# Last down matrices loaded and multiplied in three column parts, squares beside the copies, and the final norm's vector applied by feature

## The chip, the cores and the metric

The kernel runs on one core of one Trainium2 chip. The metric is the device time of one execution in microseconds (us), the median of several runs of the same program. Below, PE is TensorE, DVE is VectorE, ACT is ScalarE, POOL is GpSimd and SP is SyncE, which here only issues DMAs.

## The reference, cut to what matters

One step of a two-layer trunk over 256 prompt tokens and 8 sample tokens (264 columns in all, d = 1024). Each layer is a mixer (retention in layer 0, gated linear attention, GLA, in layer 1) and a mixture of 64 experts, eight of them for each token. The change sits at the end of both expert stages and in the norm after the second.

```python
def trunk(x, c, ...):
    for i in range(DEPTH):                       # DEPTH = 2
        sh1, sc1, g1, sh2, sc2, g2 = jnp.split(silu(c) @ ada_w[i] + ada_b[i], 6, axis=-1)
        h = modulate(x, norm_mix_g[i], sh1, sc1)          # rmsnorm(x, g) * (1 + scale) + shift
        m, S = mixer(h, ...)
        x = x + g1[:, None, :] * m
        h = modulate(x, norm_ffn_g[i], sh2, sc2)
        f = moe_ffn(h, ...)     # sum over 8 of 64 experts: w * (silu(h @ wg) * (h @ wu)) @ wd
        x = x + g2[:, None, :] * f
    return rmsnorm(x, final_norm_g), ...
def rmsnorm(x, g):
    return x * lax.rsqrt(jnp.mean(x * x, axis=-1) + EPS) * g
```

## The kernel before

**Layout.** The stream x lies feature by feature: eight chunks of 128 features (`k.x[:, c, :]`), each 264 columns, one for each token. Weights come from HBM through a ring of 12 slots of 1 MB. SP issues the loads in one fixed order, waiting for a slot to be free; `ring_full` and `ring_free` are its semaphores. All of them go through one hardware DMA queue.

**An expert stage.** Sixteen rounds of four experts. The last three rounds are light: each expert has at most 32 token slots, and the four of them stand side by side in one 128-row tile. In a light round PE computes gate (L2440), then spreads the round before back to the tokens, then up (L2440, L2557), turns the hidden tile (L2517), and multiplies by the four down matrices (L2450, weights 128x32, 512 columns at a time). ACT copies the rows out of PSUM.

**The last round** differs. Its down matrices come in two column halves (`rounds_sync`, L2350: four loads of 512 columns, then four more; `s_first_half` counts the first four). `pe_round` multiplies the first half into PSUM bank 6, ACT copies it (L3029), and `last_spread` (L2486) turns it into token columns, chunk by chunk: 128 features for each matmul, into two PSUM banks in turn, so that chunk c waits until DVE has added chunk c-2. The add is `add_last` on DVE, three instructions (L2859, L2861, L2864). After four chunks PE multiplies the second half into bank 7, ACT copies it, and the last four chunks follow.

**What follows each chunk.** PE puts `follow(c)` between the chunks. In layer 0 this is `nxt.sum` (L543), the sum of the squares for the next norm; ACT makes the squares (L526) after its second copy. In layer 1 it is `final_rows` (L1951): three transposes for each chunk (128, 128 and 8 tokens) put x by token into PSUM banks 2 to 7.

**The end of layer 0.** After the sums PE computes one block of conditioning vectors (L478), DVE and ACT finish the norm (L560, L532, L562, L569, L537), and the GLA projections (L1394) start on the first of twelve 1 MB loads of `gla_w_in`. SP has issued these behind the last down loads, two small loads (`gla_w_a`, L1335 and L1336) and four of `ada_w` (L303).

**The end of the program** (`final`). ACT squares the token rows out of PSUM with a running sum (L1959, four times 512 columns), and the samples by feature (L3433); PE sums the samples' squares (L1967). DVE puts the means together (L1999 to L2001), ACT takes the root (L1987), DVE the reciprocal (L2004). DVE then makes four blocks of 128x512 outputs, each the rows times their factor times the norm's vector (L2010); SP stores each (L2031). The samples go another way: ACT scales them (L1989), POOL multiplies by the vector (L2018), ACT issues the store (L1992). The vector itself has been loaded as 1 MB, spread over all partitions (`final_gain`, the last entry of the load plan). An empty Sqrt (L3424) ahead of all this loads ACT's table for it.

Of the kernel before, what the change touches and what calls it, by code (L numbers as in the profile page):

```python
# [217 lines left out]
def plan_loads(inp):  # L218
# [51 lines left out]
    plan.append(("final_gain", inp["final_norm_g"].rearrange("(p k n) -> p k n", p=1, k=1).to_broadcast([P, 2, D])))  # L270
# [1677 lines left out]
def final_rows(k, pe, c):  # L1948

    for t, (t0, n) in enumerate(TOKENS):  # L1950
        mm = k.nc.tensor.transpose(k.ps[0:n, 2 + 2 * t + c // 4, (c % 4) * P:(c % 4 + 1) * P], k.x[:, c, t0:t0 + n],  # L1951
                                   k.ident)
    return mm


def final_squares(k, half, sums, junk):

    for t in range(2):
        ins = k.nc.scalar.activation(junk[:, 2 * half + t, :], k.ps[:, 2 + 2 * t + half, :], ACT.Square, scale=D ** -0.5,  # L1959
                                     accum_out=sums[:, 2 * half + t:2 * half + t + 1])  # L1960
    return ins


def final_small(k, pe, small):

    for c in range(DC):
        mm = k.nc.tensor.matmul(k.ps[0:NS, 0, 0:1], small[:, c, :], k.ones[:, 0:1], start=(c == 0), stop=(c == DC - 1))  # L1967
    return mm


def final(k, behind):
    nc, out = k.nc, k.out
    s_ms, s_rt, s_rs, s_half, s_scaled, s_small, s_st = (k.sem(f"y_{n}") for n in (
        "meansq", "root", "rstd", "half_rows", "samples_scaled", "samples", "stored"))
    y = k.scratch[:, 0:TT * D].rearrange("p (t d) -> p t d", t=TT)
    scaled = k.scratch[:, TT * D:TT * D + D]
    meansq, root, rstd = (k.scratch[:, (TT + 1) * D + 4 * i:(TT + 1) * D + 4 * i + TT] for i in range(3))
    sums = behind.sums
    n_gain = k.stage["final_gain"]
    gain = slot(k, n_gain, D)[:, 0, :]  # L1980

    with nc.Block() as block:
        @block.scalar
        def _(act):
            behind.scalar(act)
            act.wait_ge(s_ms, 1)
            nc.scalar.activation(root, meansq, ACT.Sqrt).then_inc(s_rt, 1)  # L1987
            act.wait_ge(s_rs, 1)
            nc.scalar.activation(scaled[0:NS, :], k.ps[0:NS, 6:8, :].rearrange("p b d -> p (b d)"), ACT.Copy,  # L1989
                                 scale=rstd[0:NS, 2:3]).then_inc(s_scaled, 1)  # L1990
            act.wait_ge(s_small, 1)
            act.dma_start(out["y_sample"].rearrange("b o d -> (b o) d"), y[0:NS, 2, :]).then_inc(s_st, 16)  # L1992

        @block.vector
        def _(v):
            behind.vector(v)
            v.wait_ge(behind.s_sums, 2)
            v.wait_ge(behind.s_final, 4)
            nc.vector.scalar_tensor_tensor(meansq[:, 0:2], sums[:, 0:2], EPS, sums[:, 2:4], ALU.add, ALU.add)  # L1999
            k.dve.link(v, nc.vector.memset(meansq[:, 2:3], 1.0))  # L2000
            nc.vector.tensor_scalar(meansq[0:NS, 2:3], k.ps[0:NS, 0, 0:1], 1.0 / D, EPS, ALU.mult, ALU.add)\  # L2001
                .then_inc(s_ms, 1)
# [3 lines left out]
            wait_slot(k, v, n_gain)  # L2006
            for t in range(2):
                for half in range(2):
                    cols = slice(half * 512, (half + 1) * 512)
                    nc.vector.scalar_tensor_tensor(y[:, t, cols], k.ps[:, 2 + 2 * t + half, :], rstd[:, t:t + 1],  # L2010
                                                   gain[:, cols], ALU.mult, ALU.mult).then_inc(s_half, 1)

        @block.gpsimd
        def _(pool):
            behind.pool(pool)
            wait_slot(k, pool, n_gain)
            pool.wait_ge(s_scaled, 1)
            nc.gpsimd.tensor_tensor(y[0:NS, 2, :], scaled[0:NS, :], gain[0:NS, :], ALU.mult).then_inc(s_small, 1)  # L2018
# [6 lines left out]
        def _(sp):  # L2025
            behind.sync(sp)
            for t in range(2):
                for half in range(2):
                    cols = slice(half * 512, (half + 1) * 512)
                    sp.wait_ge(s_half, 2 * t + half + 1)  # L2030
                    sp.dma_start(out["y_prompt"][0, t * P:(t + 1) * P, cols], y[:, t, cols]).then_inc(s_st, 16)  # L2031
# [5 lines left out]
def experts(k, layer):  # L2037
# [108 lines left out]
    small = acc.rearrange("p c t -> p (c t)")[:, 4 * 512:].rearrange("p (c s) -> p c s", c=DC)  # L2146
    junk = acc.rearrange("p c t -> p (c t)")[:, 0:4 * 512].rearrange("p (j n) -> p j n", j=4)
    sums = heaviest[:, 0:4]
# [34 lines left out]
    s_first_half = k.sem(f"{tag}_last_down_first_halves_loaded")  # L2183
    if layer == 0:
        nxt = Norm(k, 1, 0, squares, rest[:, 0, 0:T], rest[:, 1, 0:T], bank=SUM_BANK)
    else:
        s_final = k.sem(f"{tag}_final_rows_then_small_squares")
# [118 lines left out]

    DOWN_BANK = (2, 6, 3, 7)
    RANKS_AT, LIST_AT = 6, 3
    THIRD_BANK = 7
    def rounds_sync(sp):  # L2310
# [33 lines left out]
        for half in range(2):  # L2344
            cols = slice(half * 512, (half + 1) * 512)
            for e in range(EPI):
                n = place("moe_w_down", e, LIGHT_PLACE)
                if half == 0:
                    sp.wait_ge(k.ring_free[n % RING], LAST + n // RING)
                sp.dma_start(slot(k, n, D)[:, :, cols], expert_weight("moe_w_down", expert_of[e])[:, :, cols])\  # L2350
                    .then_inc(s_first_half if half == 0 else k.ring_full[n % RING], 16)
# [119 lines left out]

    def last_spread(pe, follow):

        d = done_tiles(LAST, 0)
        pe.wait_ge(s_htc, LAST + 1)
        for half in range(2):
            if half:
                wait_light(pe, LAST, "moe_w_down")
                four_down(0, LIGHT_BLOCKS, 1, LIGHT_PLACE)
                if follow:  # L2480
                    follow(pe, 0)
                    follow(pe, 1)
            pe.wait_ge(s_part, 2 * d + 1 + half)
# [985 lines left out]
```

## Time and profile before

| | us |
|---|---|
| median of 3 runs | 1586.08 (1584.92 to 1588.89) |
| the profiled execution | 1585.7 |
| its span in the profile | 1583.9 |
| PE busy in the span | 1492.9 (94%) |
| DVE busy | 701.7 (44%) |
| ACT busy | 357.8 (23%) |
| POOL busy | 92.0 (6%) |
| mean DMA rate | 366 GB/s |

Between the span and the time of the profiled execution lie 1.8 us that no engine record shows. PE's busy time overstates its load, since its matmuls are pipelined, so the places that matter are read from stretches of the timeline, not from these shares.

### The profile page before, as it was taken

How to read it: one execution, taken by the hardware profiler on the slowest of the kernel's cores; microseconds unless marked ns; L12 is line 12 of the kernel's file. 1: busy time of each engine (PE TensorE's matmuls, PEld its weight loads, DVE VectorE, ACT ScalarE, POOL GpSimd, SP SyncE). 2: the span in 40 equal slices, each digit the busy share in tenths (PEclk: the TensorE clock that was granted, in tenths of full speed). 3: DMA queues.
4: the chain of work that ended last, by engine and by line, in shares of the span. 5: the costliest groups of instructions: out<-in, count | busy, mean ns of one | idle time of the engine just before them, and what ended most of it. 6: DMA issues, size and time to landing. Idle time of an engine off the chain costs nothing. (4 is left out here: it accounts for less than half of the span.)

```text
span 1583.9 us, 29421 instructions
## 1 busy us (share of the span) xinstructions
PE 1492.9 (94%) x11132; PEld 983.6 (62%) x11132; DVE 701.7 (44%) x1998; ACT 357.8 (23%) x760; POOL 92.0 (6%) x117
## 2 busy tenths in 40 slices
PE   6999998999999999999996899999999999999976
PEld 4778765687665566566553587777566566565533
DVE  3204534315465535534354335453754544543543
ACT  3012443203212111111120255431111211211111
POOL 0000100001000000010000000001000000010000
PEclk9999999999999999999998999999999999999998
DMA  9997699429999999999999983999999999999996
GB/s 364 389 370 267 251 399 399 177 106 359 382 418 420 421 420 420 420 419 419 415 389 415 355 285 109 352 361 338 415 418 421 420 420 420 421 418 415 392 411 245
DMA packets 153295, 580.27 MB, mean 366 GB/s; under 512 B 16893, under 2 KB 62113, under 8 KB 104938
## 3 DMA queue, kind: packets, MB, share of 16 engines
q1 hardware_dynamic: 137642, 535.74, 85.5%
q0 software_dynamic: 14912, 40.91, 6.7%
q10 hardware_dynamic: 640, 2.26, 0.4%
q8 instruction: 64, 1.05, 0.3%
q14 instruction: 37, 0.30, 0.1%
HBM read 566.12 MB, written 26.90 MB: 374 GB/s over the span
## 5 line engine op out<-in xcount | busy, mean ns | idle before, releaser
L2544 PE MATMUL ps<-ring,scratch 128*64 128x256 f32 x3008 | 330.6, 380 | 1.3 <-DMA ring<-in_moe_w_up 1.2
L2544 PEld LDWEIGHTS ps<-ring,scratch 128*64 128x64 f32 x3008 | 215.5, 137 | 106.6 <-issue 3.0
L2603 PE MATMUL ps<-ring,scratch 128*64 128x512 f32 x816 | 186.8, 598 | 1.2 <-DVE scratch L2961 0.9
L716 PE MATMUL ps<-hT,ring 128*128 128x264 f32 x768 | 182.1, 392 | 1.3 <-ACT hT L401 1.3
L2501 PE MATMUL ps<-scratch 128*128 128x264 bf16 x1344 | 165.8, 276 | 3.7 <-DVE xT L2864 2.0
L716 PEld LDWEIGHTS ps<-hT,ring 128*128 128x128 f32 x768 | 146.8, 193 | 31.6 <-issue 2.8
L2889 DVE SCALAR_TENSOR_TENSOR scratch<-scratch,ps 128x256 f32<-128x256 f32 x60 | 28.8, 480 | 300.3 <-ACT scratch L2998 279.7
L2501 PEld LDWEIGHTS ps<-scratch 128*128 128x128 bf16 x1344 | 116.7, 97 | 53.7 <-issue 15.4
L2856 DVE TENSOR_TENSOR scratch<-scratch,ps 128x264 f32<-128x264 f32 x224 | 95.3, 428 | 65.0 <-PE ps L2501 64.9
L2603 PEld LDWEIGHTS ps<-ring,scratch 128*64 128x64 f32 x816 | 53.3, 136 | 107.0 <-issue 75.1
L2998 ACT ACTIVATE scratch<-ps 128x256 f32<-128x256 f32 x60 | 23.1, 384 | 390.9 <-PE ps L2544 319.6
L2248 POOL DMA_INDIRECT scratch<-h_rows,scratch x58 | 57.7, 995 | 868.1 <-DVE scratch L2242 819.7
L3031 ACT CAST scratch<-ps 128x512 bf16<-128x512 f32 x112 | 65.5, 587 | 145.4 <-PE ps L2603 125.9
L2961 DVE TENSOR_TENSOR scratch<-ps,scratch 128x512 f32<-128x512 f32 x112 | 76.8, 686 | 37.4 <-ACT scratch L3031 37.4
L1394 PE MATMUL ps<-hT,ring 128*128 128x264 f32 x384 | 88.9, 386 | 1.2 <-ACT hT L537 1.2
L1394 PEld LDWEIGHTS ps<-hT,ring 128*128 128x128 f32 x384 | 72.0, 190 | 14.3 <-DMA ring<-in_gla_w_in 1.6
L2949 DVE TENSOR_TENSOR scratch<-scratch 128x512 bf16<-128x512 f32 x112 | 77.5, 692 | 3.9
L2407 PE MATMUL ps<-tab,scratch 128*128 128x128 f32 x464 | 62.9, 278 | 11.7 <-DVE scratch L2764 9.0
L2440 PE MATMUL ps<-ring,scratch 128*32 128x256 f32 x768 | 50.6, 422 | 17.3 <-DMA ring<-in_moe_w_gate 9.3
L2407 PEld LDWEIGHTS ps<-tab,scratch 128*128 128x128 f32 x464 | 50.2, 141 | 23.8 <-DVE scratch L2764 15.2
L2764 DVE COPY scratch<-ps 128x512 f32<-128x512 f32 x58 | 40.1, 691 | 56.1 <-PE ps L2407 56.1
L973 DVE SCALAR_TENSOR_TENSOR ring<-ring,rstd 128x512 f32<-128x512 f32 x64 | 41.3, 687 | 50.6 <-ACT rstd L1126 31.7
(411 smaller groups left out, 1538.5 us busy)
## 6 DMA issues: line engine op xcount, KB each, us to landing
ring<-in_moe_w_up SPq DMA_DIRECT2D x128, 1024.0 KB, 19.0
ring<-in_moe_w_gate SPq DMA_DIRECT2D x124, 1024.0 KB, 18.1
ring<-in_moe_w_down SPq DMA_DIRECT2D x118, 1024.0 KB, 15.5
ring<-in_ada_w SPq DMA_DIRECT2D x48, 1024.0 KB, 12.5
ring<-in_ret_w_in SPq DMA_DIRECT2D x24, 1024.0 KB, 16.8
ring<-in_state_ret SPq DMA_DIRECT2D x16, 1024.0 KB, 14.6
out_ret_sample<-ring POOLq DMA_DIRECT2D x16, 1024.0 KB, 9.0
ring<-in_gla_w_in SPq DMA_DIRECT2D x12, 1024.0 KB, 11.9
```

Source lines behind the costliest of these rows:

```text
L716: mm = nc.tensor.matmul(k.ps[:, bank, 0:T], w[:, c, m * P:(m + 1) * P], k.h[:, c, :], start=(c == 0), stop=(c == DC - 1))
L1394: mm = nc.tensor.matmul(k.ps[:, bank, 0:T], w[:, c, m * P:(m + 1) * P], k.h[:, c, :], start=(c == 0), stop=(c == DC - 1))
L2248: pool.indirect_dma_start(xtok_of(p), None, h_rows[:, :], bass.IndirectOffsetOnAxis(ap=rows[:, p:p + 1], axis=0), bounds_check=ABSENT - 1, ...
L2407: mm = nc.tensor.transpose(k.ps[:, b, c * P:(c + 1) * P], xtok_of(p)[:, d0:d0 + P], ident)
L2440: mm = nc.tensor.matmul(k.ps[lo:lo + 32, bank, j * DE:(j + 1) * DE], xg_of(p)[:, c, lo:lo + 32], slot(k, n, DE)[:, c, :], start=(c == 0), ...
L2501: mm = nc.tensor.matmul(k.ps[:, c % 2, 0:T], parts_of(p)[:, s, c * P:(c + 1) * P], slot_token[:, p, :], start=(p == 0 and s == 0), stop=(p ...
L2544: mm = nc.tensor.matmul(k.ps[lo:lo + CAP, 2 + p, j * DE:(j + 1) * DE], xg[:, p, c, lo:lo + CAP], w[:, c, :], start=(c == 0), stop=(c == DC ...
L2603: mm = nc.tensor.matmul(k.ps[lo:lo + CAP, 6 + half, :], hid_t[:, p, m, lo:lo + CAP], w[:, m, half * 512:(half + 1) * 512], start=(m == 0), ...
L2856: nc.vector.tensor_tensor(acc[:, c, :], acc[:, c, :], k.ps[:, c % 2, 0:T], ALU.add).then_inc(s_add, 1)
L2949: nc.vector.tensor_tensor(parts_of(p)[:, 2, cols], rest[:, half], parts_of(p)[:, 1, cols], ALU.subtract).then_inc(s_part, 1)
L2961: nc.vector.tensor_tensor(rest[:, half], k.ps[:, 6 + half, :], parts_of(p)[:, 0, cols], ALU.subtract).then_inc(s_rest, 1)
L3031: nc.scalar.copy(parts_of(p)[:, 0, cols], k.ps[:, 6 + half, :]).then_inc(s_rhi, 1)
```

## The change

Five things change.

1. The last round's down matrices are loaded and multiplied in three column parts, 0 to 512, 512 to 768 and 768 to 1024 (`LAST_PARTS`), in both layers. Twelve loads take the place of eight; those of the last two parts have rows of 1 KB in place of 2 KB. PE does chunks 0 and 1, then part 1, chunks 2 and 3, part 2, then the rest.
2. ACT squares chunks 0 and 1 beside its copies (`BESIDE_COPIES`); the other six come after the empty Sqrt, in layer 0 too.
3. In layer 1 DVE multiplies each finished chunk of x by the final norm's vector, one factor for each partition (`gain`, into `gained`), behind the next chunk's add.
4. `x_rows` transposes `gained` for the two prompt tiles alone, and PE sums the squares with one-column matmuls (`squares_sum`). ACT no longer reads token rows for squares. The samples' transposes stand behind the loop.
5. In `final` each output block is PSUM rows times one factor per row: DVE makes three, ACT the fourth and the samples. POOL has nothing to do, and the 1 MB load of the vector is gone.

```diff
-    plan.append(("final_gain", inp["final_norm_g"].rearrange("(p k n) -> p k n", p=1, k=1).to_broadcast([P, 2, D])))
...
+            to, of, scale = rows(1, 1)
+            nc.scalar.activation(to, of, ACT.Copy, scale=scale).then_inc(s_last, 1)
+            nc.scalar.activation(y[0:NS, 2, :], k.ps[0:NS, 0:2, :].rearrange("p b d -> p (b d)"), ACT.Copy,
+                                 scale=rstd[0:NS, 2:3]).then_inc(s_last, 1)
+            act.wait_ge(s_last, 2)
...
-            nc.vector.scalar_tensor_tensor(meansq[:, 0:2], sums[:, 0:2], EPS, sums[:, 2:4], ALU.add, ALU.add)
+            nc.vector.tensor_scalar(meansq[0:NS, 2:3], k.ps[0:NS, 6, 1:2], EPS, None, ALU.add)
+            nc.vector.tensor_scalar(meansq[:, 0:2], k.ps[:, 6:8, 0:1].rearrange("p b n -> p (b n)"), EPS, None, ALU.add)                .then_inc(s_ms, 1)
...
-                    nc.vector.scalar_tensor_tensor(y[:, t, cols], k.ps[:, 2 + 2 * t + half, :], rstd[:, t:t + 1],
-                                                   gain[:, cols], ALU.mult, ALU.mult).then_inc(s_half, 1)
+            for t, half in ((0, 0), (0, 1), (1, 0)):
+                to, of, scale = rows(t, half)
+                nc.vector.tensor_scalar(to, of, scale, None, ALU.mult).then_inc(s_half, 1)
...
+    BESIDE_COPIES = 2
+    LAST_PARTS = [(0, 512, 6, 0), (512, 768, 7, 0), (768, 1024, 7, 256)]
...
+        for i, (c0, c1, _, _) in enumerate(LAST_PARTS):
+            cols = slice(c0, c1)
             for e in range(EPI):
                 n = place("moe_w_down", e, LIGHT_PLACE)
+                if i == 0:
                     sp.wait_ge(k.ring_free[n % RING], LAST + n // RING)
                 sp.dma_start(slot(k, n, D)[:, :, cols], expert_weight("moe_w_down", expert_of[e])[:, :, cols])\
+                    .then_inc((s_first_half, s_third_quarter, k.ring_full[n % RING])[i], 16)
...
     def last_spread(pe, follow):
...
+        chunk(0)
+        chunk(1)
+        pe.wait_ge(s_third_quarter, 16 * EPI)
+        last_down(1)
+        chunk(2)
+        chunk(3)
+        wait_light(pe, LAST, "moe_w_down")
+        pe.wait_ge(s_part, 2 * d + 2)
+        last_down(2)
+        for c in range(4, DC):
+            if c == 6:
+                pe.wait_ge(s_part, 2 * d + 3)
+            if follow and c == 4:
+                follow(pe, 0)
+                follow(pe, 1)
+            chunk(c)
+            if follow:
+                follow(pe, c - 2)
...
+    def squares_sum(t, c):
+
+        t0, n = TOKENS[t]
+        nc.tensor.matmul(k.ps[:, 6 + t, 0:1], final_sq[:, c, t0:t0 + n], ones[:, 0:1], start=(c == 0),
+                         stop=(c == DC - 1))
+
     def x_rows(pe, c):
 
+        pe.wait_ge(s_gained, c + 1)
+        for t, (t0, n) in enumerate(TOKENS[0:2]):
+            nc.tensor.transpose(k.ps[:, 2 + 2 * t + c // 4, (c % 4) * P:(c % 4 + 1) * P], gained[:, c, t0:t0 + n], ident)
+        pe.wait_ge(s_squares, c + 1)
+        squares_sum(0, c)
+        for b in range(DC // 2 + 1) if c == DC // 2 else range(c, c + 1) if c > DC // 2 else ():
+            squares_sum(1, b)
...
+            nc.scalar.copy(last_rows[:, c0:c1], k.ps[:, bank, at:at + c1 - c0]).then_inc(s_part, 1)
+            if beside and i < BESIDE_COPIES:
+                act.wait_ge(s_add, DC * (LAST + 1) + i + 1)
+                beside(act, i)
...
+                if beside and c:
+                    v.wait_ge(s_add, DC * (LAST + 1) + c)
+                    beside(c - 1)
...
         nc.scalar.activation(silu[0:1, 0, 0:1], ident[0:1, 0:1], ACT.Sqrt)
+        for c in range(BESIDE_COPIES, DC):
+            act.wait_ge(s_add, DC * (LAST + 1) + c + 1)
+            square(act, c)
```

The program of PE at the end of layer 1, before: behind the first half (first row) come four chunks (L2486), the second half, two chunks' transposes (L1951), and then chunk and transposes in turn.

```order
L2450 MATMUL ps<-ring,scratch 32x512 x8
L2486 MATMUL ps<-scratch 128x264 x4
L2450 MATMUL ps<-ring,scratch 32x512 x8
L1951 MATMUL ps<-tab,xT 128x128 x2
L1951 MATMUL ps<-tab,xT 8x128
L1951 MATMUL ps<-tab,xT 128x128 x2
L1951 MATMUL ps<-tab,xT 8x128
L2486 MATMUL ps<-scratch 128x264
```

The same place now, where L2457 is the down matmul, L2470 a chunk, L2519 the transposes and L2512 a one-column sum of squares:

```order
L2457 MATMUL ps<-ring,scratch 32x512 x8
L2470 MATMUL ps<-scratch 128x264 x2
L2457 MATMUL ps<-ring,scratch 32x256 x8
L2470 MATMUL ps<-scratch 128x264 x2
L2457 MATMUL ps<-ring,scratch 32x256 x8
L2519 MATMUL ps<-tab,scratch 128x128 x2
L2512 MATMUL ps<-tab,scratch 128x1
L2519 MATMUL ps<-tab,scratch 128x128 x2
L2512 MATMUL ps<-tab,scratch 128x1
L2470 MATMUL ps<-scratch 128x264
L2519 MATMUL ps<-tab,scratch 128x128 x2
L2512 MATMUL ps<-tab,scratch 128x1
```

Half of the second half's matmuls has moved ahead of chunks 2 and 3, and sums stand between the transposes and the chunks. Further down, PE's rows from the fifth chunk's `follow` to the end now read:

```order
L2519 MATMUL ps<-tab,scratch 128x128 x2
L2512 MATMUL ps<-tab,scratch 128x1 x6
L2470 MATMUL ps<-scratch 128x264
L2519 MATMUL ps<-tab,scratch 128x128 x2
L2512 MATMUL ps<-tab,scratch 128x1 x2
...
L3338 UNCONDITIONAL_BRANCH
L3342 MATMUL ps<-tab,scratch 8x128 x8
L3345 MATMUL ps<-tab,scratch 8x1 x8
```

Six sums at once (one of the first tile, five of the second) stand ahead of the last chunk, and the samples' eight transposes ahead of their sum (the last row; L1967 before).

ACT at the end of layer 1, before, from the copies of the two halves on:

```order
L3029 COPY scratch<-ps 128x512 x2
L3422 UNCONDITIONAL_BRANCH
L3424 ACT_TABLE_LOAD
L3424 ACTIVATE scratch<-tab 1x1
L1959 ACTIVATE scratch<-ps 128x512 x2
L3433 ACTIVATE scratch<-xT 128x64
L1959 ACTIVATE scratch<-ps 128x512 x2
```

And now, where L3041 is a copy of a part and L3429 a square of one chunk:

```order
L3041 COPY scratch<-ps 128x512
L3429 ACTIVATE scratch<-xT 128x256
L3041 COPY scratch<-ps 128x256
L3429 ACTIVATE scratch<-xT 128x256
L3041 COPY scratch<-ps 128x256
L3464 UNCONDITIONAL_BRANCH
L3466 ACT_TABLE_LOAD
L3466 ACTIVATE scratch<-tab 1x1
L3429 ACTIVATE scratch<-xT 128x256 x6
```

Two squares have moved in between the copies; the other six stand behind the table load, and PE's sums wait for them. In layer 0 ACT has the same order now (squares of 128x264), where before all eight squares stood ahead of its table load.

## Rows read from the trace of the kernel before

**Rows 1.** The chain of waits, two of its last pieces: start us, us, what.

```profile
1543.18 18.14 DMA ring<-in_moe_w_down
1561.46 3.22 PE ps L2450 x16
```

**Rows 2.** Timeline at the end of layer 1: start us, us, engine, instructions, [idle before].

```profile
1564.72 0.59 ACT L3029 COPY scratch<-ps 128x512 f32<-128x512 f32 x1 [4.54 <-PE ps L2450]
...
1565.40 1.13 PE L2486 MATMUL ps<-scratch 128*128 128x264 f32 x4 [0.73 <-issue]
...
1566.12 0.17 DVE L2859 TENSOR_TENSOR scratch<-ps,mod 128x8 f32<-128x8 f32 x1 [6.91 <-PE ps L2486]
...
1566.60 0.16 DVE L2864 TENSOR_TENSOR xT<-scratch,xT 128x8 f32<-128x8 f32 x1
...
1567.99 1.92 PE L2450 MATMUL ps<-ring,scratch 128*32 128x512 f32 x16
...
1570.67 1.28 ACT L3424 ACT_TABLE_LOAD   x1
...
1571.96 0.20 ACT L3424 ACTIVATE scratch<-tab 1x1 f32<-1x1 f32 x1
...
1576.49 0.16 DVE L1999 SCALAR_TENSOR_TENSOR scratch<-scratch 128x2 f32<-128x2 f32 x1 [2.08 <-ACT scratch L1959]
```

**Rows 3.** The same timeline, from the factors on to the last store.

```profile
1577.32 1.10 ACT L1989 ACTIVATE scratch<-ps,scratch 8x1024 f32<-8x1024 f32 x1 [0.24 <-DVE scratch L2004]
1577.32 2.73 DVE L2010 SCALAR_TENSOR_TENSOR scratch<-ps,scratch,ring 128x512 f32<-128x512 f32 x4
1578.10 2.58 SPq L2031 DMA_DIRECT2D out_y_prompt<-scratch  x4
1578.58 2.33 POOL L2018 TENSOR_TENSOR scratch<-scratch,ring 8x1024 f32<-8x1024 f32 x1 [60.00 <-ACT scratch L1989]
1580.94 0.58 ACTq L1992 DMA_DIRECT2D out_y_sample<-scratch  x1
```

**Rows 4.** Windows: stretch, us, busy us (instructions) of PE, PEld, DVE, ACT, POOL, clock, DMA share, GB/s.

```profile
1582.50:1583.00 0.50, 0.00 (x0) 0.00 (x0) 0.00 (x0) 0.00 (x0) 0.00 (x0) 0.50 0.07 25
```

**Rows 5.** Timeline of PE and its weight loads (PEld) at the end of layer 1.

```profile
1571.47 0.30 PEld L2486 LDWEIGHTS ps<-scratch 128*128 128x128 f32 x2
...
1572.03 0.49 PE L1951 MATMUL ps<-tab,xT 128*128 128x128 f32 x3
...
1575.35 0.45 PEld L1967 LDWEIGHTS ps<-tab,scratch 128*8 128x8 f32 x16 [0.64 <-ACT scratch L3433]
```

**Rows 6.** DVE groups by form: busy us, mean ns of one, idle before.

```profile
L594 DVE CAST scratch<-scratch 32x256 bf16<-32x256 f32 x4 | 1.1, 284 | 0.1
```

**Rows 7.** Timeline from the end of layer 0 into the GLA projections.

```profile
884.59 0.61 PE L2486 MATMUL ps<-scratch 128*128 128x264 f32 x2
...
893.87 3.30 ACT L537 ACTIVATE hT<-hT,mod 128x256 f32<-128x256 f32 x8 [3.05 <-DVE hT L569]
...
894.52 7.36 PE L1394 MATMUL ps<-hT,ring 128*128 128x264 f32 x32 [1.17 <-ACT hT L537]
```

**Rows 8.** The first load of gla_w_in: issue (ns), who waited for it (us), landing (us).

```profile
L303 SPq DMA_DIRECT2D ring<-in_gla_w_in x1: 470/470/470, 879.9 to 879.9; - x1
...
  PEld ps L1394: 1.6, 1
...
DMA to landing us min/median/max: 14.4/14.4/14.4
```

**Rows 9.** The last round's down loads, both layers: duration ns of an issue, min/median/max.

```profile
L2350 SPq DMA_DIRECT2D ring<-in_moe_w_down x16: 543/1077/5085, 854.0 to 1554.2; - x16
```

**Rows 10.** Windows, columns as in rows 4: last down loads, then gla_w_in, then the last layer's.

```profile
874.00:880.00 6.00, 4.42 (x26) 2.00 (x26) 1.37 (x8) 0.96 (x2) 0.00 (x0) 1.00 0.90 286
904.00:924.00 20.00, 19.87 (x88) 15.35 (x87) 4.79 (x10) 8.87 (x12) 0.00 (x0) 1.00 1.10 348
1556.00:1562.00 6.00, 3.63 (x58) 1.92 (x54) 0.48 (x1) 0.37 (x1) 0.00 (x0) 1.00 1.05 388
```

More of the change, by code:

```diff
@@ L1943, in gla, with rows, store @@
     release_semaphores(k, old)
[L1948 to L1968, printed above, removed]
 def final(k, behind):
     nc, out = k.nc, k.out
-    s_ms, s_rt, s_rs, s_half, s_scaled, s_small, s_st = (k.sem(f"y_{n}") for n in (
-        "meansq", "root", "rstd", "half_rows", "samples_scaled", "samples", "stored"))
+    s_ms, s_rt, s_rs, s_half, s_last, s_st = (k.sem(f"y_{n}") for n in (
+        "meansq", "root", "rstd", "half_rows", "last_half_rows", "stored"))
     y = k.scratch[:, 0:TT * D].rearrange("p (t d) -> p t d", t=TT)
-    scaled = k.scratch[:, TT * D:TT * D + D]
     meansq, root, rstd = (k.scratch[:, (TT + 1) * D + 4 * i:(TT + 1) * D + 4 * i + TT] for i in range(3))
-    sums = behind.sums
-    n_gain = k.stage["final_gain"]
-    gain = slot(k, n_gain, D)[:, 0, :]
+    def rows(t, half):
+        return y[:, t, half * 512:(half + 1) * 512], k.ps[:, 2 + 2 * t + half, :], rstd[:, t:t + 1]
+    def store(eng, t, half):
+        eng.dma_start(out["y_prompt"][0, t * P:(t + 1) * P, half * 512:(half + 1) * 512], rows(t, half)[0])\
+            .then_inc(s_st, 16)
     with nc.Block() as block:
@@ L2026, in _ @@
             behind.sync(sp)
[L2027 to L2031, printed above, removed]
+            sp.wait_ge(s_half, 1)
+            store(sp, 0, 0)
+            sp.wait_ge(s_last, 1)
+            store(sp, 1, 1)
+            sp.wait_ge(s_half, 2)
+            store(sp, 0, 1)
+            sp.wait_ge(s_half, 3)
+            store(sp, 1, 0)
             sp.wait_ge(s_st, 16 * 5)
@@ L2186, in experts @@
     else:
-        s_final = k.sem(f"{tag}_final_rows_then_small_squares")
+        s_final, s_gained, s_squares = (k.sem(f"{tag}_final_{n}") for n in ("sums", "gained", "squares"))
     h_done = k.sem(f"{tag}_heavy_step")
@@ L2594, in pe_round @@
                 wait_light(pe, r, "moe_w_down")
-            for half in range(1 if last else 2):
+            if last:
+                last_down(0)
+            for half in range(0 if last else 2):
                 four_down(0, LIGHT_BLOCKS, half, LIGHT_PLACE)
@@ L3327, in tail_vector, with gain, finish @@
         rounds_vector(v)
-        def finish():
+        def gain(c):
+            nc.vector.tensor_scalar(gained[:, c, :], k.x[:, c, :], k.fin_g[:, c:c + 1], None, ALU.mult)\
+                .then_inc(s_gained, 1)
+        def finish(beside=None):
             vector_round(v, LAST)
@@ L3374, in tail_vector @@
                         .then_inc(x_add, 1)
+            if layer:
+                v.wait_ge(x_add, pairs * DC + DC)
+                for c in range(DC):
+                    gain(c)
             v.br(done)
@@ L3377, in tail_vector @@
         with nc.body(usual, valid_engines=here):
-            finish()
+            finish(gain if layer else None)
             v.br(done)
@@ L3382, in tail_vector, with square @@
             nxt.vector(v)
+    def square(act, c):
+        if layer == 0:
+            nxt.square(act, c)
+        else:
+            nc.scalar.activation(final_sq[:, c, :], k.x[:, c, 0:TP], ACT.Square, scale=D ** -0.5).then_inc(s_squares, 1)
     def tail_scalar(act):
```

108 lines of the change are left out of this document (46 added, 62 removed).

## The prediction

> **What bounds the kernel now.** I read the chain of waits first, because it says where a saving counts. In its last 40 us it goes through a load: the fourth of the first four down loads of layer 1 is issued at 1543.18, lands 18.14 us later, and PE starts the last round's down matmuls at 1561.46 [rows 1]. Nothing of the change stands ahead of that moment in layer 1, so I take it as a fixed point and ask how long the rest takes: 1583.9 less 1561.46, or 22.4 us. Next I read the timeline from there. The reader is to see PE as the thread: copy, four chunks, second half at 1567.99 with no wait named [rows 2], chunks and transposes in turn, the samples' sum; DVE puts the means together at 1576.49 [rows 2]; at 1577.32 the factors are there (call that moment T), and what follows are outputs and stores [rows 3]. So there are two pieces, 1561.46 to T and T to the end, 15.9 and 6.6 us. For layer 0 I looked at what starts the GLA projections at 894.52. PE's row names ACT [rows 7], but its weight load waited 1.6 us for the first load of gla_w_in, issued at 879.9 and landed 14.4 us later, at 894.3 [rows 8]. ACT's first chunk starts at 893.87 and takes 0.41 (eight in 3.30) [rows 7], so it is done at 894.3 as well. Both gates open together: an earlier norm gains nothing there, a later load costs its whole delay.
>
> **Layer 0.** The squares beside the copies and the earlier chunks move the norm forward: by the same order of steps as worked out for layer 1 below, chunk 4, at 884.59 [rows 7], would come some 2 us earlier, of which the table load takes back more than half. None of it counts while the load is the gate. The load is later: the last two parts move 2.1 MB in rows of 1 KB. Rows of 1 KB ran at 348 GB/s (gla_w_in), rows of 2 KB at 388 [rows 10]. 2.1 MB take 6.03 us at the one and 5.41 at the other, so all that is queued behind lands 0.6 us later: 894.9, and PE starts at about 895.0 in place of 894.52, **0.5 us late**. PE is then busy without a break [rows 10], so nothing gives this back. SP has four more issues ahead of the small loads; each of these took 0.54 to 5.1 us, the middle one 1.08 [rows 9]. I cost them at nothing, since the queue holds some ten us of transfers when they are issued. With that cover gone they cost four times 1.08, 4.3 us. Bounds: 0 and 4.9.
>
> **A rule on the rows.** The Trainium skill, DMA: Bandwidth & Descriptors, section Specifications, asks for transfers of 512 B or more for line rate. By it, rows of 1 KB would be no slower than rows of 2 KB and layer 0 would cost nothing. The trace disagrees, 348 against 388 GB/s [rows 10], so I keep 0.5.
>
> **Layer 1 up to the last part.** Prices first. A chunk holds PE 0.45 us (two in 1.13 with the tail of the last) and takes 1.36 from its start to x added, 1565.40 to 1566.76 [rows 2]. A down part of 256 columns takes half of 1.92, so 0.95 with its tail, 0.92 on PE. A copy of 256 columns takes some 0.37, from 0.59 for 512. An add takes 0.62 (three instructions, 1566.12 to 1566.76, the next begins a little earlier), and a result of PE reaches another engine about 0.28 after PE has moved on (1566.12 less 1565.40 less 0.45) [rows 2]. Now the order: copy done at 1565.31, chunk 0 at 1565.40, two chunks to 1566.30, part 1 to 1567.22, chunks 2 and 3 to 1568.12. The old second half began at 1567.99 [rows 2], so half of it is already done when the other half starts: part 2 runs 1568.12 to 1569.04, where the old one ended at 1569.91. The load of part 2 is in by then: the whole second half was there at 1567.99, and 0.6 more gives 1568.6 at the worst, a wait of up to 0.5, which I take as 0. **So far 0.8 us are won.**
>
> **The loop after it.** The two `follow`s need two transposes each, 0.11 on PE (three in 0.49, of which some 0.16 is the tail of the last) [rows 5], and one sum. A one-column sum with 128x128 weights does not occur in the trace in f32. The lower bound is the samples' sum with 8-column weights: 16 weight loads in 0.45, 0.026 each, 0.05 for a sum's two passes [rows 5]. The upper one is two whole weight loads of 0.19, 0.38. Where two loads of this size follow each other they take 0.30, the second 0.11 behind the first [rows 5]; that is the nearest row, and I take two of these, **0.21 a sum**. Then 0.43 a follow, chunk 4 from 1569.90 to 1570.35. Now the first new wait: follow 2 needs square 2. ACT copies part 2 at 1569.32 to 1569.69, then loads the table, 1.28, and runs the empty Sqrt, 0.20 [rows 2], then a square, 0.45 with its signal: 1571.62. PE has stood since 1570.56, 1.06 us, and chunk 5 is behind that wait: it starts at 1571.83. Before, the load lay beside PE's work (1570.67 to 1571.96) and no square was behind it. Follow 3 and chunk 6 end at 1573.16. Follow 4 waits 0.3 for DVE, whose add of 0.62 has the gain of one chunk before it; the gain I take as 0.27 on DVE (a one-source operation of 256 columns took 0.284 [rows 6]; between 0.16, the 8-column add of rows 2, and that the end moves 0.3). Then follow 4 has six sums, 1.29, and chunk 7 starts at 1574.96. Follow 5 takes 0.64; follow 6 waits 0.5 for the gain behind the last add, and ends at 1577.22; follow 7 at 1577.87. Eight transposes of the samples take 0.86, their sum 0.45, to 1579.17. DVE starts at 1579.45 in place of 1576.49 [rows 2]; from there to T are 0.83 in the old and 0.75 in the new form. **T = 1580.2, 2.9 us later.** In words: PE's sums cost 16 times 0.21, 3.4 us, on PE's path, where before ACT's squares from PSUM cost only what came after the last transposes.
>
> **From T to the end.** Before: ACT 1.10, POOL 2.33, then the samples' store at T + 3.62 [rows 3]. The last bytes moved just after 1582.5 [rows 4], and the end came at T + 6.58. Now POOL's step is gone: ACT does a prompt block (0.7) and the samples, the store is issued at T + 1.9, and with the same 2.96 from issue to end it would close at T + 4.9. DVE needs three blocks of 0.68 (four took 2.73 [rows 3]), so the last prompt store goes out at T + 2.15. The first goes out at T + 0.78, its bytes start 0.8 later, 1 MB at 388 GB/s takes 2.7, and about 1.05 lie between the last bytes and the end: T + 5.35. That bounds it; **1.2 us are won**, end at 1585.55 against 1583.9.
>
> **Sum.** Layer 1 ends 1.65 later (2.88 to T, less 1.23 behind it), layer 0 adds 0.5: 2.15 us. The profiled execution had 1585.7, so 1587.85, given as 1587.8. That is 0.4 below the median shown, so the forecast is 1.7 us, 0.11%, over the median; 0.3%, or 4.8 us, is about what a measurement of this kernel can tell from no change.
>
> **Rivals.**
> - The sums are cheap, 0.05 (weight loads hidden). For it: the samples' sum [rows 5]. Against it: the second load stands 0.11 behind the first there. T falls by 1.7: 1586.1. Chance 0.18.
> - The sums cost 0.38. T rises by 2.0: 1589.8. Chance 0.07.
> - Slower by more than can be missed: in layer 0 SP's four more issues delay the small loads and `ada_w` while the queue runs dry. For it: the queue was already not full there, 286 GB/s in place of 388 [rows 10]. Against it: a load lands over ten us after its issue, so its start is covered. Price up to 4.3 on top: 1592.1. It decides from 3.0 us on. Chance 0.08; half of that price, 1590, another 0.05.
> - Faster than before: without the 1 MB load of the vector the first four down loads of layer 1 land sooner, since the engines share their time. The fourth took 18.14 us [rows 1]; if 2.5 of these go, 1585.3. It is a gain from 1.7 on. Against it: the vector's load is issued behind all of them. Chance 0.10.
> - Rows of 1 KB run as fast as rows of 2 KB: layer 0 is level, 1587.3. Chance 0.10. This is the rule named above.
> - The engine drains after a table load for as long again. Against it: the empty Sqrt starts at 1571.96, right behind the load [rows 2]. The squares would come 1.4 later, all behind them too: 1589.2. Chance 0.03. The Trainium skill, ScalarE: Activation LUTs, section What ACT_TABLE_LOAD costs, puts a drain of about 1.38 us behind each switch; the row shows none.
> - The parts don't do what they are for: the last part lands after 1569.0 and PE waits as before. The 0.8 is lost: 1588.6. Chance 0.04.
>
> **How the numbers follow.** My forecast, 1587.8, has 0.35 and a range of its own from 1586.6 to 1589.0. The range for all is 1585.0 to 1590.6: it holds all but the far queue case, part of the near one, and part of the case on the faster side. Faster by over 0.3% would need several of the gains at once, 0.04; slower by over 0.3% is the queue case and the upper end of the dear sums, 0.09; the rest is 0.87.
>
> **What would show each step.** Right: PE's wait for ACT of about 1 us ahead of the third sum; six one-column sums between transposes and the last chunk, in about 1.3 us; the samples' sum some 3 us later after the first down matmul than before; no POOL row at the end, and 5.4 us from the factors to the end; in layer 0 the projections' first weights waiting for their load, at 895. Wrong: sums that follow each other at 0.05, a first projection at 897 or later, or a last round whose first down matmul comes well before 1561.5 plus what layer 0 added.

## The result

The changed kernel takes 1591.66 us in the median (16 runs, 1588.92 to 1595.40), the kernel before 1586.01 beside it: a ratio of 1.0035, with a 95% interval from 1.0025 to 1.0045, so 4.0 to 7.1 us slower. I had forecast 1587.8. The profiled execution took 1591.17, with a span of 1589.3 against 1583.9.

I use three marks below. **F** is the start of the first chunk matmul of layer 1's last round (PE L2470, before L2486), **T** the start of DVE's output blocks, as in the prediction, and **D** the way from the first down matmul of layer 0's last round to F. Before, F is 1565.40 [rows 2] and T 1577.32 [rows 3]: 11.92 us, and 6.58 to the end. The timeline of PE in the changed kernel, from the first down part on:

```profile
1565.25 1.92 PE L2457 MATMUL ps<-ring,scratch 128*32 128x512 f32 x16 [0.46 <-ACT scratch L3021]
1567.93 1.13 PE L2470 MATMUL ps<-scratch 128*128 128x264 f32 x4 [0.75 <-issue]
1568.99 1.07 PE L2457 MATMUL ps<-ring,scratch 128*32 128x256 f32 x16
1569.99 1.16 PE L2470 MATMUL ps<-scratch 128*128 128x264 f32 x4
1571.08 1.07 PE L2457 MATMUL ps<-ring,scratch 128*32 128x256 f32 x16
1572.08 0.44 PE L2519 MATMUL ps<-tab,scratch 128*128 128x128 f32 x2
1572.35 0.28 PE L2512 MATMUL ps<-tab,scratch 128*128 128x1 f32 x2
1572.49 0.42 PE L2519 MATMUL ps<-tab,scratch 128*128 128x128 f32 x2
...
1574.54 0.38 PE L2512 MATMUL ps<-tab,scratch 128*128 128x1 f32 x2 [0.74 <-ACT scratch L3429]
...
1576.74 1.40 PE L2512 MATMUL ps<-tab,scratch 128*128 128x1 f32 x12
1578.00 0.69 PE L2470 MATMUL ps<-scratch 128*128 128x264 f32 x2
...
1579.96 0.50 PE L2512 MATMUL ps<-tab,scratch 128*128 128x1 f32 x4
1580.32 0.41 PE L2519 MATMUL ps<-tab,scratch 128*128 128x128 f32 x2
...
1580.94 1.03 PE L3342 MATMUL ps<-tab,scratch 128*8 128x128 f32 x8
1581.90 0.55 PE L3345 MATMUL ps<-tab,scratch 128*8 128x1 f32 x16
```

Here are the one-column sums (L2512) between the transposes (L2519). One alone holds PE for 0.14 us (1572.49 less 1572.35), six in a row for 1.26 (1578.00 less 1576.74), a pair for 0.36 (1580.32 less 1579.96). The third waits 0.74 us for its square. The chain of waits in the same stretch shows why: behind the last copy it runs through the table load.

```profile
1572.29 0.37 ACT scratch L3041
1572.66 0.02 issue
1572.68 1.28 ACT L3466
1573.96 0.01 issue
1573.97 0.20 ACT scratch L3466
1574.18 0.32 ACT scratch L3429
1574.49 0.04 issue
1574.54 0.38 PE ps L2512 x2
```

The timeline of the other engines from T, and the windows of the last 6 us (granted clock, DMA share and GB/s are the last three columns):

```profile
1583.25 0.69 ACT L1969 ACTIVATE scratch<-ps,scratch 128x512 f32<-128x512 f32 x1 [0.24 <-DVE scratch L1983]
1583.25 2.07 DVE L1987 TENSOR_SCALAR scratch<-ps,scratch 128x512 f32<-128x512 f32 x3
1584.03 2.05 SPq L1958 DMA_DIRECT2D out_y_prompt<-scratch  x4
1584.96 0.58 ACTq L1973 DMA_DIRECT2D out_y_sample<-scratch  x1
```

```profile
1584.00:1586.00 2.00, 0.00 (x0) 0.00 (x0) 1.32 (x3) 0.93 (x1) 0.00 (x0) 0.68 0.55 205
1586.00:1588.00 2.00, 0.00 (x0) 0.00 (x0) 0.00 (x0) 0.00 (x0) 0.00 (x0) 0.50 0.95 308
1588.00:1590.00 2.00, 0.00 (x0) 0.00 (x0) 0.00 (x0) 0.00 (x0) 0.00 (x0) 0.50 0.08 32
```

T is 1583.25, so F to T takes 15.32 us, 3.40 more than before; T to the end takes 6.05, 0.53 less. F itself comes 2.53 later. That makes the 5.4 us between the two spans. The 2.53 would be 1.3 more if the clock had been alike: in the kernel before, the first down part of layer 1's last round took 3.22 us [rows 1] (granted clock 0.50 from 1562 to 1565), here 1.92. In layer 0, the instructions on `gla_w_in` (its first load alone) show the gate: PE itself waits for it, where before only its weight load did [rows 8]. In this one profile the load takes no longer than before (14.1 us, 14.4 before).

```profile
L302 SPq DMA_DIRECT2D ring<-in_gla_w_in x1: 520/520/520, 880.3 to 880.3; - x1
...
  PE ps L1393: 1.4, 1
...
DMA to landing us min/median/max: 14.1/14.1/14.1
```

### The profile page after: what moved, and what is told of

The parts are those of the page before. It is cut to its first block and busy times, and to the rows that moved or that the text cites. A ratio compares the mean times of both kernels' runs of the same rounds, so it can differ in the third digit from the quotient of the medians.

```text
span 1589.3 us, 29577 instructions
## 1 busy us (share of the span) xinstructions
PE 1497.9 (94%) x11196; PEld 988.3 (62%) x11196; DVE 703.2 (44%) x2005; ACT 359.4 (23%) x763; POOL 89.5 (6%) x116
## 3 DMA queue, kind: packets, MB, share of 16 engines
q8 instruction: 65, 1.06, 0.3%
## 6 DMA issues: line engine op xcount, KB each, us to landing
ring<-in_ret_w_in SPq DMA_DIRECT2D x24, 1024.0 KB, 17.2
ring<-in_state_ret SPq DMA_DIRECT2D x16, 1024.0 KB, 14.1
```

## Experiments

**The theories.** S: the cost is the new final norm, whose sums and waits hold PE in layer 1's tail. U: the cost lies ahead of F, in layer 0's parts and what they delay. N: what was lost ahead of F is chance of that one execution. C came up on the way: the clock. I put three switches into the changed kernel: PARTS lists the layers whose last down matrices come in three parts, BESIDE_ON those whose first two squares stand beside the copies, NEW_FINAL chooses the norm. All off is the kernel before, all on the changed one.

Here is what every kernel gave. D and F to T are read from PE's and DVE's timeline as above; the last column says whether the granted clock fell to 0.50 (1.2 GHz) between F and PE's last matmul. The changed kernel was profiled three times (the first, after_again, after_third). Kernels with one number in the second column had one execution, beside one of 1585.68 of the kernel before.

| kernel | ratio (95%) or us | D | F to T | clock fell |
|---|---|---|---|---|
| before | | 690.42 | 11.92 | no |
| changed, first profile | 1.0035 (1.0025 to 1.0045) | 692.52 | 15.32 | no |
| layer0_only | 1.0008 (0.9994 to 1.0022) | 690.79 | 11.92 | no |
| layer1_only | 1.0045 (1.0029 to 1.0061) | 690.54 | 17.14 | yes |
| final_only | 1.0033 (1.0017 to 1.0049) | 690.39 | 17.78 | yes |
| parts_only | 1.0014 (1.0005 to 1.0024) | 693.72 | 11.38 | no |
| sums_doubled | 1.0061 (1.0046 to 1.0076) | 691.21 | 20.51 | yes |
| sums_first_only | 1.0017 (1.0008 to 1.0027) | 692.83 | 13.33 | no |
| table_late | 1.0024 (1.0010 to 1.0037) | 692.84 | 14.34 | no |
| pool_adds | 1.0002 (0.9989 to 1.0015) | 691.39 | 12.81 | no |
| after_again | 1.0029 (1.0019 to 1.0040) | 691.54 | 16.20 | yes |
| l0_two_loads | 1.0019 (1.0006 to 1.0032) | 691.18 | 11.91 | no |
| four_sums | 1.0018 (1.0004 to 1.0032) | 690.34 | 13.31 | no |
| sums_wide | 1.0029 (1.0019 to 1.0039) | 691.73 | 15.45 | no |
| narrow_doubled_b | 1593.0 | 691.78 | 21.30 | yes |
| wide_doubled_a | 1597.42 | 693.59 | 17.92 | no |
| wide_doubled_b | 1593.75 | 691.00 | 18.37 | no |
| after_third | 1589.06 | 689.97 | 17.24 | yes |
| l1_parts_old_norm | 0.9997 (0.9983 to 1.0011) | 690.12 | 11.38 | no |

**Which part costs.** Four kernels, each with some of the switches on.

```diff
+PARTS, BESIDE_ON, NEW_FINAL = (0,), (0,), False      # layer0_only
+PARTS, BESIDE_ON, NEW_FINAL = (1,), (1,), True       # layer1_only
+PARTS, BESIDE_ON, NEW_FINAL = (), (1,), True         # final_only
+PARTS, BESIDE_ON, NEW_FINAL = (0, 1), (0,), False    # parts_only
```

> The change in layer 0 alone (three column parts and squares beside the copies there); layer 1 and the final norm as before. Theory U (the 3.8 us that the changed kernel's profile had lost before layer 1's last round comes from layer 0's parts): some 3.8 us slower, 1589.8 beside 1586.0, with PE's first down matmul of the last round near 1565. Theory N (that loss is chance of one execution, the rest is the tail of layer 1): within 0.5 us of the kernel before, first down matmul near 1561.5.

> The change in layer 1 and the final norm alone; layer 0 as before. Theory U: only the tail's own cost stays, 2.9 us to the factors less some 0.5 behind them, 2.4 us over the kernel before. Theory N: all that the change costs stays, 4 to 5.6 us, so the tail must lose more than its own rows show, or the removed load of the final vector changes something ahead. A third way (the tail as I summed it): 1.65 us.

> The new final norm alone (gained copies, squares, one-column sums on PE, by-feature output), the last down matrices in two halves in both layers. If the sums on PE are the cost and the parts a gain of 0.8 us, the tail loses 2.9 + 0.8 - 0.5, 3.2 us over the kernel before. If the parts are the cost, it is within 0.5 us of the kernel before.

> The three column parts in both layers and the squares beside the copies in layer 0, with the old final norm. If the sums on PE are the cost: 0.8 us faster than the kernel before (the parts' own gain), or level. If the parts are the cost, in layer 0's loads or in the rounds between: 2 to 4 us slower.

The two kernels with the new norm and without layer 0's parts are slower by 4.6 to 9.7 and by 2.7 to 7.8 us; their D is that of the kernel before, within 0.2. So the new norm costs in the tail and U alone falls: layer1_only was to lose 2.4 by U and 4 to 5.6 by N. layer0_only can't be told from level (1.0 us faster to 3.5 slower), where U asked for 3.8. But F to T is 17.1 and 17.8 in the two kernels with the new norm, not 15.3. PE's timeline at the end of final_only shows what is different from the changed kernel's first profile:

```profile
1580.80 0.67 PE L2653 MATMUL ps<-tab,scratch 128*128 128x128 f32 x2
1581.26 0.85 PE L2640 MATMUL ps<-tab,scratch 128*128 128x1 f32 x4
1581.97 1.87 PE L3487 MATMUL ps<-tab,scratch 128*8 128x128 f32 x8
```

The same matmuls took 0.41, 0.50 and 1.03 there: from 1579.6 on the granted clock is 0.50. This is theory C. The parts win in layer 1 as was expected (11.38 in place of 11.92 with the old norm), yet parts_only is 0.8 to 3.8 us slower: its D is 3.3 longer. In layer 0, the first load of `gla_w_in` in layer0_only and PE's first projections in parts_only:

```profile
  PE ps L1395: 1.9, 1
...
DMA to landing us min/median/max: 15.0/15.0/15.0
```

```profile
895.74 9.07 PE L1395 MATMUL ps<-hT,ring 128*128 128x264 f32 x32 [1.90 <-DMA ring<-in_gla_w_in]
```

The load lands later, PE stands 1.9 us, and in parts_only the clock falls right behind that wait (0.79 in the mean of 892 to 900), so that 32 matmuls take 9.07 us, where they took 7.39 in the changed kernel's first profile.

A second wait belongs to layer 0's new order and stands in no expectation. It lies in the GLA stage, where ACT first reads PSUM for the outer products of the samples (L1813 in the kernel before, then three rows of the changed kernel, where it is L1812):

```profile
960.52 0.84 ACT L1813 ACTIVATE rstd<-ps,scratch 128x256 f32<-128x256 f32 x2 [0.62 <-PE ps L1415]
```

```profile
964.85 0.84 ACT L1812 ACTIVATE rstd<-ps,scratch 128x256 f32<-128x256 f32 x2 [3.23 <-issue]
965.75 0.39 PE L1414 MATMUL ps<-scratch,pick 96*128 96x512 bf16 x1 [0.72 <-ACT rstd L1812]
q14 instruction: 1, 0.01, 0.6%
```

In all 14 kernels that have the parts and the early squares in layer 0 (l0_two_loads among them) ACT stands there for 2.9 to 3.2 us, for nothing that the profile names, and PE then waits 0.4 to 0.7 us for it; in the five others ACT stands 0.62 us, for PE. In each of the 14 a single packet of the instruction queue q14 moves in that stretch (the last row is the DMA view from 961.6 to 964.85), in the five none. So ACT may be waiting for its own program; no run separates that, nor the parts from the early squares.

**What in the norm costs.** Four edits of the changed kernel.

```diff
 def squares_sum(t, c):
-    nc.tensor.matmul(k.ps[:, 6 + t, 0:1], final_sq[:, c, t0:t0 + n], ones[:, 0:1], start=(c == 0), stop=(c == DC - 1))
+    for i in range(2):                                   # sums_doubled
+        nc.tensor.matmul(k.ps[:, 6 + t, 0:1], final_sq[:, c, t0:t0 + n], ones[:, 0:1],
+                         start=(c == 0 and i == 0), stop=(c == DC - 1 and i == 1))
+    if c == 0:                                           # sums_first_only
+        nc.tensor.matmul(k.ps[:, 6 + t, 0:1], final_sq[:, c, t0:t0 + n], ones[:, 0:1], start=True, stop=True)
```

```diff
 # table_late and pool_adds, layer 1
-nc.scalar.activation(silu[0:1, 0, 0:1], ident[0:1, 0:1], ACT.Sqrt)
 for c in range(BESIDE_COPIES, DC):
     square(act, c)
+    if c == DC - 2:
+        nc.scalar.activation(silu[0:1, 0, 0:1], ident[0:1, 0:1], ACT.Sqrt)
 # pool_adds also; PE then makes one sum for each tile, after the samples' transposes
+for c in range(1, DC):
+    nc.gpsimd.tensor_tensor(final_sq[:, 0, :], final_sq[:, 0, :], final_sq[:, c, :], ALU.add)
```

> The changed kernel with each of layer 1's 16 one-column sums of squares made twice (the means come out doubled). Theory S (the sums hold PE on the path that sets the end, some 0.14 us each at full clock): the time from the last round's first chunk to the factors, 15.3 us at full clock, grows by 16 x 0.14 = 2.2 us; if a sum costs the 0.21 that I predicted, by 3.4. Rival W (PE waits for squares and gains anyway, the sums lie in those waits): under 1 us. Theory C (the longer PE works behind the last rounds, the more of it meets a fallen clock): the granted clock is down in the samples' transposes, and up to 2 us more on top.

> The changed kernel with only the first of eight chunks summed (14 of layer 1's 16 sums left out, so the means are wrong); all waits stay. Theory S: first chunk to factors falls by 14 x 0.14 = 2.0 us, to 13.3, and the whole by 2 to 4, to 1588 to 1589.7. Rival W: under 0.7 us. Theory C: the clock stays up through the samples' transposes (1.0 us for eight, not 1.9).

> The changed kernel with layer 1's empty root, which loads the table, moved behind the seventh square, where the scalar engine idled 1.9 us. If PE's wait for the third square (0.74 us) is paid in full on the path: first chunk to factors falls by 0.7 us, to 14.6. If the gains on the vector engine set the pace behind it: by 0 to 0.3.

> The changed kernel with the table loaded late, and the squares of layer 1 added up over the chunks on GpSimd, so that PE makes two sums in place of 16 and waits for no square between chunks. Theory S: first chunk to factors falls by the 14 sums, 2.0 us, and by the waits, to about 12.5 to 13 (the old norm had 11.9), the whole to about 1588.5. Rival: an add of 256 columns on GpSimd takes over 1 us (its 1,024 columns took 2.33), the chain of seven is late, and the factors come no sooner than now.

Without 14 of the sums F to T is 13.33, 1.99 less, as theory S had it. The empty root behind the seventh square takes 0.98 off, more than the wait of 0.74 that it removes. With the adds on GpSimd (five of them in a row took 4.40 us) it is 12.81, and the kernel can't be told from the one before (1.7 us faster to 2.4 slower). Doubled sums add 5.2 us, not 2.2, because the clock falls again:

```profile
1583.52 1.87 PE L3343 MATMUL ps<-tab,scratch 128*8 128x128 f32 x8
```

**A second profile, the rows of 1 KB, four sums, wide sums.** l0_two_loads keeps three parts in layer 0's work, but loads the second column half whole (four loads in place of eight). four_sums has layer 0 as before; in layer 1 GpSimd adds the squares of chunks 0 to 6, and PE makes four sums at the very end.

```diff
 # l0_two_loads, layer 0: loads in two halves, work in three parts
-pe.wait_ge(s_third_quarter, 16 * EPI)
+wait_light(pe, LAST, "moe_w_down")
 last_down(1)
 # four_sums, PE at the end
+pe.wait_ge(s_added, DC - 2)
+for c in (0, DC - 1):
+    nc.tensor.matmul(k.ps[:, 6 + t, 0:1], final_sq[:, c, t0:t0 + n], ones[:, 0:1], start=(c == 0), stop=(c == DC - 1))
 # sums_wide
-nc.tensor.matmul(k.ps[:, 6 + t, 0:1], final_sq[:, c, t0:t0 + n], ones[:, 0:1], start=(c == 0), stop=(c == DC - 1))
+nc.tensor.matmul(k.ps[:, 6 + t, 0:P], final_sq[:, c, t0:t0 + n], ones, start=(c == 0), stop=(c == DC - 1))
```

> The changed kernel once more, unchanged, for a second profile. Theory C (the clock falls in the new tail in many executions, and the first profile happened to be without it): about even chances that the eight samples' transposes take 1.9 us (half clock) in place of 1.0; then 17 to 18 us from the first chunk to the factors, otherwise 15.3 again. Rival (the changed kernel always has 15.3, the other kernels' falls were their own): 15.3 us and full clock.

> The change in layer 0 alone, still worked in three column parts with the squares beside the copies, but its second column half loaded whole, in rows of 2 KB. If the rows of 1 KB are what makes gla_w_in late: the first projection is no longer held by its load and starts 19.1 us after the last round's first down matmul (20.05 with the 1 KB rows, 19.54 in the kernel before), and the whole is level with the kernel before or 0.4 us faster. If the loads are late for another reason: 20 us again.

> Layer 0 as in the kernel before; layer 1 with the three parts and the new norm, but the squares of chunks 0 to 6 added up on GpSimd, four sums on PE at the end, the samples' sum ahead of them, and the table loaded late. From the GpSimd kernel's 12.8 us between first chunk and factors less the samples' sum (0.45) and the last add (0.7, half of it hidden): 12.0, where the kernel before has 11.9. With 6.05 behind it, 0.4 us faster than the kernel before in its profile, 1585.3: no difference that the times can show. Rival: the table load or the adds are late again, 13 us and some 0.6 slower.

> The changed kernel with each of layer 1's 16 sums made 128 columns wide (the ones matrix in place of one of its columns). Theory C2 (stretches of one-column matmuls count as little work and let the clock fall): clock full through the samples' transposes; a sum costs a few hundredths more, first chunk to factors 15.5 to 16.5. Rival: the clock falls as before, 17 us or more. One profile can't settle it, since the changed kernel's own first profile had no fall either.

The second profile has the fall, at the samples' transposes; 16.20 us is less than the 17 to 18 said for it. In l0_two_loads the first load of `gla_w_in` lands 14.1 us after its issue, as in the kernels without parts. That speaks for the rows of 1 KB as what makes it late, but it is one profile, and the changed kernel's first one had 14.1 with them. The kernel gains nothing, and is 1.0 to 5.1 us slower than the one before: PE now waits 1.37 us for the whole second half, and the first projection waits for ACT, 20.18 us after the first down matmul; ACT's later stand is there too. four_sums misses its 12.0 and is 0.6 to 5.1 us slower: PE's eight narrow matmuls (two for each f32 sum) stand at the very end and take 1.05 us.

```profile
1577.80 1.05 PE L3498 MATMUL ps<-tab,scratch 128*128 128x1 f32 x8
```

sums_wide is at full clock, which settles nothing alone, as its expectation says. The times don't show what the fall costs: sums_wide and after_again, measured together, have the same ratio, 1.0029.

**Is the fall of the clock the change's own?** Both kernels below keep PE busy equally long; the sums are doubled in both, one column wide (narrow_doubled_b, the kernel of sums_doubled) or 128 (wide_doubled_a and _b, sums_wide with each sum made twice, so its means come out doubled too).

> The changed kernel with each of layer 1's 16 sums made twice, one column wide (the means come out doubled), a second look. Theory C2 (the fall of the clock in the tail goes with the stretches of one-column sums): the clock falls to half before PE is done, as in the first look, and first chunk to factors is 18.5 us or more. Rival (the fall depends on chance alone): as likely full clock, 17.0.

> The same with the doubled sums 128 columns wide, first look. Theory C2: full clock until PE is done, first chunk to factors 17.2 to 17.7 us although PE works as long as with the narrow sums. Rival: the clock falls as with the narrow ones, 18.5 us or more.

> The same kernel as the one before, second look: both looks at full clock by C2, at least one at half clock by the rival.

> The changed kernel, unchanged, a third look. C2 and the rival alike leave open whether the clock falls here (first look: after PE was done, second look: in the samples' transposes); 15.3 us from first chunk to factors if not, 16 to 17.5 if so.

Windows of the tail, PE's busy time first, granted clock third from the end; narrow, then wide:

```profile
1574.00:1576.00 2.00, 2.00 (x17) 1.88 (x18) 0.00 (x0) 0.00 (x0) 0.00 (x0) 1.00 0.00 0
1576.00:1578.00 2.00, 2.00 (x12) 2.00 (x11) 1.17 (x6) 0.56 (x2) 0.00 (x0) 0.50 0.00 0
1578.00:1580.00 2.00, 2.00 (x12) 2.00 (x12) 0.00 (x0) 0.00 (x0) 0.00 (x0) 0.50 0.00 0
```

```profile
1582.00:1584.00 2.00, 2.00 (x19) 1.88 (x18) 0.05 (x1) 0.00 (x0) 0.00 (x0) 1.00 0.00 0
1584.00:1586.00 2.00, 2.00 (x20) 1.93 (x19) 1.11 (x6) 0.56 (x2) 0.00 (x0) 1.00 0.00 0
1586.00:1588.00 2.00, 2.00 (x21) 1.77 (x19) 0.00 (x0) 0.00 (x0) 0.00 (x0) 1.00 0.00 0
```

PE is busy in both, and the clock falls with the narrow sums alone. (At full clock the two wide kernels take 17.92 and 18.37 us from F to T, over the 17.2 to 17.7 that was said; in the second one PE waits 0.42 us for a down load.) Over all profiles: with narrow sums between the chunks it fell between F and PE's end in six of eight, with wide sums in none of three, with the few or none of sums_first_only, pool_adds and four_sums in none of three, with the old norm in none of five. So the fall belongs to the change. When it comes differs from profile to profile; in the changed kernel's third it took the last two pairs of sums as well:

```profile
1575.63 0.66 PE L2519 MATMUL ps<-tab,scratch 128*128 128x128 f32 x2 [0.43 <-DVE scratch L3355]
1576.08 0.85 PE L2512 MATMUL ps<-tab,scratch 128*128 128x1 f32 x4
1576.80 0.67 PE L2519 MATMUL ps<-tab,scratch 128*128 128x128 f32 x2
...
1577.97 1.87 PE L3342 MATMUL ps<-tab,scratch 128*8 128x128 f32 x8
```

**Layer 1's parts alone,** with the old norm:

```diff
+PARTS, BESIDE_ON, NEW_FINAL = (1,), (), False        # l1_parts_old_norm
```

> The three column parts in layer 1 alone, with the old final norm; layer 0 as in the kernel before. If the parts gain in layer 1 and cost in layer 0: first chunk to factors 11.4 us in place of 11.9, from layer 0's last first down matmul to layer 1's first chunk 690.4 us as in the other kernels without layer 0's parts (691.9 in the mean with them), and 0.5 us faster than the kernel before, which the times cannot tell from level. If the parts cost in layer 1's loads as well: 691.5 us or more, and level to 1 us slower.

D is 690.12 and F to T 11.38: the parts gain 0.54 us in layer 1 and cost nothing ahead of it. The five kernels without layer 0's parts have a D from 690.12 to 690.54 (two of them, this one and the kernel before, with 1.3 to 1.4 us of it in a first down part at half clock); the 13 with them have 689.97 to 693.72, in the mean 691.92, 1.55 more; with that down part at full clock in all five, it would be 2.1 more. This is the quickest kernel of the study by its median (1583.52 beside 1585.52), though the interval, 0.9983 to 1.0011, can't tell it from the kernel before.

## Why the prediction was wrong

The direction was right, the size less than half of what came. The forecast was 2.15 us over the profile before; by the rows it is 1.55 up to F (the mean of the 13 kernels with layer 0's parts; the changed kernel's own three profiles give 0.92), 4.33 from F to T (16.25 in the mean of those three, less 11.92) and -0.5 behind T, 5.4 in all. The two timings gave 4.0 to 7.1 and 3.0 to 6.3. The 3.2 us that were missed are four terms: 1.05 in layer 0, 0.93 for the clock between F and T, 0.52 for the rest of that stretch, 0.7 behind T. Step by step:

- **Layer 0, "0.5 us late" and "nothing gives this back".** The load is about as forecast: it lands 14.8 us after its issue in the mean of 13 kernels with the parts, 14.2 in five without; 0.6 was said. PE's first projection comes 0.35 us later after the first down matmul (19.80 against 19.45). **The first step that failed is that this late start was taken as the whole price of layer 0:** D is 1.55 longer. ACT's stand in the GLA stage makes the way from the first projection to the router of layer 1's experts 0.6 to 0.9 us longer where no clock falls (161.8 to 162.1 against 161.2); the prediction has no such wait. In five of 13 profiles the clock also fell between 892 and 908, behind PE's wait for the load, in none of the five without; another fall, around 915 to 921, came in two of five and three of 13. At 1.7 us a fall by parts_only's row (9.07 against 7.39), all of these make 0.4 more with the parts. The half clock in two first down parts of the five takes 0.5 off again. The remaining 0.6 or so I did not settle: it lies in the expert rounds, where PE's waits for `in_moe_w_up` differ from profile to profile (0.3 us in the kernel before, 2.4 in parts_only, but 0.8 in layer1_only as well).
- **"So far 0.8 us are won."** The parts win 0.54 (parts_only, l1_parts_old_norm). A part of 256 columns holds PE 1.0 us, not 0.92, and two chunks 1.06 to 1.09, not 0.90, so part 2 begins 3.15 us after F, where 2.72 was forecast.
- **The sums, "0.21 a sum".** Right in a row (1.26 for six), too dear for one alone (0.14). The rival of 0.05 is refuted, that of 0.38 holds only at half clock (after_third, a pair in 0.72). Leaving 14 out frees 1.99.
- **The wait for square 2, 1.06.** It is 0.74, for the reason given. The Trainium skill, ScalarE: Activation LUTs, section What ACT_TABLE_LOAD costs, adds a drain of about 1.38 us to the load; here the load starts 0.02 us after the copy and the root 0.01 after the load, so the trace disagrees once more.
- **"T = 1580.2, 2.9 us later".** F plus 14.8 was forecast; at full clock it is F plus 15.3. **The second step that failed is that this piece was priced at one clock.** No rival named a fall of the clock in PE's new work, and by F to T it costs 0.9 us in the second profile and 1.9 in the third, 0.93 in the mean of the three.
- **T to the end, 5.35.** It is 6.05. I let the 1 MB of stores run at 388 GB/s, a rate of loads; they ran at 308 (the window from 1586 to 1588 above), 3.4 us in place of 2.7, and that is the 0.7. It could have been read ahead: in the kernel before the window from 1580 to 1582, when the stores run, has 311.
- **The rivals.** "The queue runs dry" named 1592.1, close to what came, by luck, for a reason that did not occur: the first load of `gla_w_in` is issued at 880.3, 0.4 later than before [rows 8]. "First down loads land sooner" is refuted: without the vector's load D is 690.34 to 690.54, and 690.42 with it. Rows of 1 KB were not as fast as rows of 2 KB: 348 against 388 GB/s [rows 10], and l0_two_loads has the load back at 14.1, though it also halves the number of these loads. The rule of the Trainium skill, DMA: Bandwidth & Descriptors, section Specifications, asks only for 512 B; the two rates of rows 10 disagree with it.

## What to carry to other kernels

Work that is moved onto the engine that leads the chain has to be priced at both of the clocks that its own trace shows, the more so where it consists of matmuls of one column between waits. Split a load into narrower columns where the split is what the next step waits for (layer 1), and not where another load stands behind it as the gate (layer 0). Compare the other engines' stands too, far behind the place that was changed: a wait can come up there that no step of the sum names. Price stores by a row of stores.

## What the runs showed of the hardware

The granted clock fell from 1.00 to 0.50 while PE was busy without a gap in the rows (2.00 of 2.00 us in each window from 1572 on in narrow_doubled_b) with one-column matmuls, and stayed at 1.00 in the same program with 128 columns. The wide sum is hardly dearer: 16 more of them took 2.47 us (17.92 less 15.45), 0.15 each. Behind an edit of ACT's program in layer 0, ACT stood 2.9 to 3.2 us without a named cause some 80 us later, in 14 kernels of 14, each time with one packet of the instruction queue; in the five without the edit it stood 0.62. The output stores ran at 308 GB/s with the DMA engines 95% busy, where loads in rows of 2 KB run at 388 [rows 10].
